# One stage each for output product, row norm and MLP in a two-block transformer kernel: tiles normed, turned and split one by one

## What is computed

```python
h = layer_norm(DN_ALPHA * h + mix, ln_mix_g[layer], ln_mix_b[layer])
h = layer_norm(DN_ALPHA * h + sq_relu_mlp(h, w_ff1[layer], w_ff2[layer]), ln_ffn_g[layer], ln_ffn_b[layer])
```

## Time and profile before

| what | value |
| --- | --- |
| median of 3 runs | 3636.25 us (3626.71 to 3639.91) |
| the profiled execution, its own time | 3637.71 us |
| its span, from first to last instruction | 3635.9 us |
| PE busy | 3322.3 us, 91% of the span |
| DVE busy | 1719.4 us, 47% |
| ACT busy | 841.4 us, 23% |
| POOL busy | 1112.7 us, 31% |
| mean granted clock of TensorE | 0.954 |

### The profile page before, as it was taken

One profiled execution on the slowest core, in us unless ns is written; L12 is line 12 of the kernel. 1 busy time (PEld: TensorE's weight loads), 2 busy tenths in 40 slices (PEclk: granted clock), 3 DMA queues, 4 the chain that ended last, 5 costly groups with the idle time before them and its releaser, 6 DMA issues. The chain is left out here.

```text
span 3635.9 us, 51954 instructions
## 1 busy us (share of the span) xinstructions
PE 3322.3 (91%) x20484; PEld 2927.8 (81%) x20484; DVE 1719.4 (47%) x3176; ACT 841.4 (23%) x1645; POOL 1112.7 (31%) x690
## 2 busy tenths in 40 slices
PE   8999999998988989799999995599998699999996
PEld 7898998887977879588888885588888688888885
DVE  4646465534776322633333347345553543333336
ACT  3545454412132110211111112133331111111110
POOL 5434343320195312523333303010001243333322
PEclk9999999888999999799999996799999799999998
DMA  6111111321001111211111101000001121111111
GB/s 192 52 46 47 46 47 52 151 60 41 30 14 38 58 33 37 81 47 46 46 47 57 58 0 36 8 22 14 10 4 58 34 71 46 46 48 55 46 35 47
DMA packets 179276, 173.28 MB, mean 48 GB/s; under 512 B 50267, under 2 KB 162331, under 8 KB 178971
## 3 DMA queue, kind: packets, MB, share of 16 engines
q1 hardware_dynamic: 177566, 170.70, 14.9%
q10 hardware_dynamic: 1568, 0.61, 0.1%
HBM read 157.30 MB, written 19.23 MB: 49 GB/s over the span
## 5 line engine op out<-in xcount | busy, mean ns | idle before, releaser
L2149 DVE TENSOR_TENSOR x<-x,banks 128x512 f32<-128x512 f32 x512 | 344.0, 684 | 210.3 <-PE banks L80 210.2
L78 PE MATMUL banks<-winbuf_hi,xt_hi 128*128 128x256 f32 x1024 | 302.1, 295 | 12.0 <-ACT qkn L950 7.5
L80 PE MATMUL banks<-winbuf_hi,xt_lo 128*128 128x256 f32 x1024 | 290.5, 284 | 0.0
L79 PE MATMUL banks<-winbuf_lo,xt_hi 128*128 128x256 f32 x1024 | 290.3, 284 | 0.0
L78 PEld LDWEIGHTS banks<-winbuf_hi,xt_hi 128*128 128x128 f32 x1024 | 196.5, 192 | 31.3 <-ACT qkn L950 11.5
L78 PE MATMUL banks<-h1t_hi,f1w_buf_hi 128*128 128x512 f32 x512 | 199.9, 390 | 2.7 <-PEq L2075 2.7
L78 PE MATMUL banks<-h3t_hi,f2w_buf_hi 128*128 128x512 f32 x512 | 199.9, 390 | 2.7 <-PEq L2075 2.7
L79 PE MATMUL banks<-h3t_lo,f2w_buf_hi 128*128 128x512 f32 x512 | 199.7, 390 | 0.0
L79 PE MATMUL banks<-h1t_lo,f1w_buf_hi 128*128 128x512 f32 x512 | 199.7, 390 | 0.0
L80 PE MATMUL banks<-h1t_hi,f1w_buf_lo 128*128 128x512 f32 x512 | 199.7, 390 | 0.0
L80 PE MATMUL banks<-h3t_hi,f2w_buf_lo 128*128 128x512 f32 x512 | 199.6, 390 | 0.0
(11 more groups left out here) (424 smaller groups left out, 8803.4 us busy)
## 6 DMA issues: line engine op xcount, KB each, us to landing
f1w_raw<-in_w_ff SPq DMA_DIRECT2D x32, 1024.0 KB, 5.2
f2w_raw<-in_w_ff SPq DMA_DIRECT2D x32, 1024.0 KB, 5.3
winraw<-in_w_in SPq DMA_DIRECT2D x128, 128.0 KB, 3.2
gluw_raw<-in_ssm_w_glu SPq DMA_DIRECT2D x16, 512.0 KB, 4.6
x<-in_x SPq DMA_DIRECT2D x8, 512.0 KB, 6.4
wow_raw<-in_w_out SPq DMA_DIRECT2D x4, 1024.0 KB, 5.1
x<-in_x SPq DMA_DIRECT2D x1, 4096.0 KB, 15.4
gew_raw<-in_w_ple_gate SPq DMA_DIRECT2D x4, 1024.0 KB, 5.0
```

The source lines that it names most:

```text
L78: nc.tensor.matmul(out, a.hi, b.hi, start=start, stop=False)
L79: nc.tensor.matmul(out, a.hi, b.lo, start=False, stop=False)
L80: return nc.tensor.matmul(out, a.lo, b.hi, start=False, stop=stop)
L2149: nc.vector.tensor_tensor(xx, xx, chip.ps[:, 4 + w % 4, :], ALU.add).then_inc(s_acc, 1)
```

## The change

`stage_product` and the "ln" kind of `stage_norm_transpose` are gone, and `stage_mlp` is one block that holds the output product (`Product`), the norm behind it (`RowNorm`), the MLP and the norm behind that. What remains of the old stage, `stage_transpose`, has its work unchanged for the callers that had no norm.

`RowNorm` works tile by tile. DVE takes the moments of tile j, makes variance plus epsilon, and centres the tile and multiplies it by the gain (`centre`). POOL takes the power for this tile alone, waits for ACT, and adds the shift (`root_and_shift`). ACT multiplies by the root (`scale`). PE turns tile j-2 behind the matmuls of tile j (`turn`), and `high_parts`, `low_parts` and `rescale` follow as before. POOL norms no tile by itself.

`Product` makes chunks 0 and 1 as before, and chunks 2 and 3 together, tile by tile, into one bank (512 columns), so that a tile's sum is complete after its 48 matmuls. Its weight has three buffers. Chunk 0 is loaded and split in the stage before: in the last part of the GLU (buffers at 160, 168, 184 and 144 KB) and in the last head of the attention.

In the MLP, hidden units 0 and 1 of chunk 0 need tiles 0 to 3 alone; they run before the turns of tiles 6 and 7. The first chunks of both MLP weights are loaded within the product. At the end, PE waits for all low parts of the last chunk, and then makes the two output units of a tile, with the turn of tile j-2 behind those of tile j. The first latent weight is loaded and split during the last chunk, the second once all hidden units are done, ahead of POOL's work for the norm. In the last norm each tile is stored once its shift is added. The addresses of several buffers move.

```diff
+    def centre(self, dve, j):
+        v, x = self.nc.vector, self.x
+        if j == 0:
+            dve.wait_ge(self.landed, 32)
+        if j >= 2:
+            dve.wait_ge(self.aggr, j - 1)
         for h in range(2):
-            self.nc.vector.bn_stats(self.st[:, h, :], x[:, j, h * HALF:(h + 1) * HALF]).then_inc(self.half, 1)
+            v.bn_stats(self.st[:, j % 2, h, :], x[:, j, h * HALF:(h + 1) * HALF]).then_inc(self.half, 1)
         dve.wait_ge(self.half, 2 * j + 2)
-        self.nc.vector.bn_aggr(self.mv[:, j, :], self.st[:, :, :].rearrange("p a s -> p (a s)")).then_inc(self.done, 1)
-        if j == NT - 1:
-            dve.wait_ge(self.done, NT)
+        v.bn_aggr(self.mv[:, j, :], self.st[:, j % 2, :, :].rearrange("p a s -> p (a s)")).then_inc(self.aggr, 1)
+        dve.wait_ge(self.aggr, j + 1)
+        v.tensor_scalar(self.rstd[:, j:j + 1], self.mv[:, j, 1:2], 1.0, LN_EPS, ALU.mult, ALU.add).then_inc(self.var, 1)
+        v.scalar_tensor_tensor(x[:, j, :], x[:, j, :], self.mv[:, j, 0:1], self.gtile[:, :],
+                               ALU.subtract, ALU.mult).then_inc(self.cen, 1)
+    def root_and_shift(self, pool, j):
+        g, x = self.nc.gpsimd, self.x
+        pool.wait_ge(self.var, j + 1)
+        g.tensor_tensor(self.rstd[:, j:j + 1], self.rstd[:, j:j + 1], self.chip.neghalf[:, :], ALU.pow).then_inc(self.root, 1)
+        pool.wait_ge(self.scaled, j + 1)
+        g.tensor_tensor(x[:, j, :], x[:, j, :], self.btile[:, :], ALU.add).then_inc(self.done, 1)
+    def scale(self, act, j):
+        act.wait_ge(self.root, j + 1)
+        act.wait_ge(self.cen, j + 1)
+        self.nc.scalar.activation(self.x[:, j, :], self.x[:, j, :], ACT.Copy,
+                                  scale=self.rstd[:, j:j + 1]).then_inc(self.scaled, 1)
+    def bank(self, j, q):
+        return self.chip.ps[:, self.banks[2 * (j % 2) + q], :]
+    def view(self, t, j, q):
+        if self.by_token:
+            return t[:, 4 * q:4 * q + 4, :].rearrange("p k (c j) -> p k c j", j=NT)[:, :, :, j]
+        return t[:, 4 * q:4 * q + 4, j * P:(j + 1) * P]
+    def turn(self, pe, j):
+        pe.wait_ge(self.done, j + 1)
+        if j >= 2:
+            pe.wait_ge(self.lo, 2 * j - 2)
+        for q in range(2):
+            for k in range(4):
+                last = self.nc.tensor.transpose(self.bank(j, q)[:, k * P:(k + 1) * P],
+                                                self.x[:, j, (4 * q + k) * P:(4 * q + k + 1) * P], self.chip.ident[:, :])
+            last.then_inc(self.turned, 1)
+    def high_parts(self, act, j):
+        for q in range(2):
+            act.wait_ge(self.turned, 2 * j + q + 1)
+            self.nc.scalar.activation(self.view(self.dst.hi, j, q), self.bank(j, q).rearrange("p (k c) -> p k c", k=4),
+                                      ACT.Copy).then_inc(self.hi, 1)
...
+    def rescale(self, act, j):
+        act.wait_ge(self.turned, 2 * j + 2)
+        self.nc.scalar.mul(self.x[:, j, :], self.x[:, j, :], ALPHA).then_inc(self.again, 1)
+    def low_parts(self, dve, j):
+        for q in range(2):
+            dve.wait_ge(self.hi, 2 * j + q + 1)
+            self.nc.vector.tensor_tensor(self.view(self.dst.lo, j, q), self.bank(j, q).rearrange("p (k c) -> p k c", k=4),
+                                         f32(self.view(self.dst.hi, j, q)), ALU.subtract).then_inc(self.lo, 1)
 def token_rows(t, h, j):
...
+    CHUNKS = D // CH
+    WIDE = 2
...
+    def sync(self, sp):
+        for n in range(1, self.CHUNKS):
+            self.ws.load(sp, n)
+    def pool(self, pool):
+        self.ws.do_split(pool, 1, 1)
+        self.ws.do_split(pool, 2, 2)
+        self.ws.do_split(pool, 3, 0, (self.mm, NT))
+    def tile(self, out, n, b, j):
+        for k in range(KT):
+            last = mm3(self.nc, out, self.rows.at(slice(None), k, slice(j * P, j * P + P)),
+                       self.ws.bufs[b].at(slice(None), k, slice(None)), k == 0, k == KT - 1)
+        return last
+    def pe(self, pe):
+        ps, norm = self.chip.ps, self.norm
+        for n in range(2):
+            pe.wait_ge(self.ws.split, n + 1)
+            for j in range(NT):
+                if n:
+                    pe.wait_ge(self.added, j + 1)
+                self.tile(ps[:, j, 0:CH], n, n, j).then_inc(self.mm, 1)
+        pe.wait_ge(self.ws.split, 4)
+        for j in range(NT):
+            pe.wait_ge(self.added, NT + j + 1 if j < 4 else self.narrow + j - 3)
+            self.tile(ps[:, j % 4, 0:CH], 2, 2, j)
+            self.tile(ps[:, j % 4, CH:2 * CH], 3, 0, j).then_inc(self.mm, 1)
+            if j == 2:
+                pe.wait_ge(self.added, self.narrow)
+            if j >= 2:
+                norm.turn(pe, j - 2)
+    def act(self, act):
+        for j in range(NT):
+            if j >= 2:
+                self.norm.high_parts(act, j - 2)
+            self.norm.scale(act, j)
+            if j >= 2:
+                self.norm.rescale(act, j - 2)
+        for j in (NT - 2, NT - 1):
+            self.norm.high_parts(act, j)
+            self.norm.rescale(act, j)
+    def dve(self, dve):
+        def add(u, cols, bank):
+            dve.wait_ge(self.mm, u + 1)
+            xx = self.x[:, u % NT, cols]
+            self.nc.vector.scalar_tensor_tensor(xx, xx, self.x_scale, bank, ALU.mult, ALU.add).then_inc(self.added, 1)
+        for u in range(self.narrow):
+            n, j = u // NT, u % NT
+            add(u, slice(n * CH, (n + 1) * CH), self.chip.ps[:, j, 0:CH])
+        for j in range(NT):
+            add(self.narrow + j, slice(HALF, D), self.chip.ps[:, j % 4, :])
+            dve.wait_ge(self.added, self.narrow + j + 1)
+            self.norm.centre(dve, j)
+            if j >= 2:
+                self.norm.low_parts(dve, j - 2)
+        for j in (NT - 2, NT - 1):
+            self.norm.low_parts(dve, j)
...
             ws.load_all(sp, KT)
+            sp.wait_ge(ws.split, KT)
+            then.load(sp, 0, first=True)
         @block.gpsimd
         def _(pool):
             ws.split_all(pool, KT, s_mm, 2)
+            then.do_split(pool, 0, 0, (s_mm, 2 * KT - 2))
...
+            product.sync(sp)
+            ws1.load(sp, 0, first=True)
+            sp.wait_ge(product.ws.split, product.CHUNKS)
             ws2.load(sp, 0, first=True)
+            sp.wait_ge(product.mm, product.narrow)
+            first.load(sp)
             with sp.Fori(1, NB) as n:
                 ws1.load(sp, n)
                 ws2.load(sp, n)
-            moments.load(sp)
+            norm.load(sp)
+            if latent is not None:
+                sp.wait_ge(s_m1, U1 * (NB - 1))
+                latent.load(sp, 0)
+                sp.wait_ge(s_m1, U1 * NB)
+                sp.wait_ge(ws2.split, NB)
+                latent.load(sp, 1)
+            if store is not None:
+                for j in range(NT):
+                    sp.wait_ge(norm.done, j + 1)
+                    sp.dma_start(store[:, j, :], x[:, j, :]).then_inc(norm.stored, 16)
+                sp.wait_ge(norm.stored, 16 * NT)
         @block.gpsimd
         def _(pool):
-            ws2.do_split(pool, 0, 0)
...
+            product.pool(pool)
+            ws1.do_split(pool, 0, 0)
+            for j in range(NT):
+                first.root_and_shift(pool, j)
+            ws2.do_split(pool, 0, 0, (product.mm, product.narrow + NT))
             ws1.do_split(pool, 1, 1)
...
+            if latent is not None:
+                latent.do_split(pool, 0)
+                latent.do_split(pool, 1)
+            for j in range(NT):
+                norm.root_and_shift(pool, j)
...
+            pe.wait_ge(ws1.split, 1)
+            pe.wait_ge(product.added, product.narrow + NT - 2)
+            pe.wait_ge(first.lo, NT)
+            hidden_unit(0, 0, 0)
+            first.turn(pe, NT - 2)
+            hidden_unit(0, 0, 1)
+            first.turn(pe, NT - 1)
+            pe.wait_ge(product.added, product.narrow + NT)
+            pe.wait_ge(first.lo, 2 * NT)
+            hidden_unit(0, 0, 2)
+            hidden_unit(0, 0, 3)
...
+            pe.wait_ge(ws2.split, NB)
+            pe.wait_ge(s_alo, U1 * NB + 2)
+            pe.wait_ge(s_sq, U1 * NB + 4)
+            for j in range(NT):
+                output_unit(NB - 1, 1, 2 * j)
+                output_unit(NB - 1, 1, 2 * j + 1)
+                if norm.dst is not None and j >= 2:
+                    norm.turn(pe, j - 2)
+            if norm.dst is not None:
+                norm.turn(pe, NT - 2)
+                norm.turn(pe, NT - 1)
...
+            for j in range(NT):
+                if norm.dst is not None and j >= 2:
+                    norm.high_parts(act, j - 2)
+                norm.scale(act, j)
+                if norm.dst is not None and j >= 2:
+                    norm.rescale(act, j - 2)
+            if norm.dst is not None:
+                for j in (NT - 2, NT - 1):
+                    norm.high_parts(act, j)
+                    norm.rescale(act, j)
...
+            for j in range(NT):
+                add(NB - 1, 2 * j)
```

(36 more changed lines are left out.)

329 lines of the change are left out of this document (85 added, 244 removed).

## The result

The changed kernel takes 3530.0 us, the median of four runs (3529.2 to 3531.3); the kernel before takes 3638.1 beside it (four runs, 3626.7 to 3640.3). The ratio is 0.971, with a 95% interval of 0.969 to 0.973. That is 108 us less, where 91.5 were forecast. The profiled executions have spans of 3635.9 and 3529.5 us, a difference of 106.4.

The account below looks back on a forecast made before the run. PE, busy for 91% of the span, bounds the kernel, so gains come only where it stands still. Four sites sum to 44 + 43 + 10 - 5.5 = 91.5 us, from 3636.25 to 3545; range 3525 to 3582.

Parts of the forecast that it names:

- site 4: Last norm, from the last hidden unit to the end: 57.2 us before, forecast 5.5 us slower.
- Site 1: From the GLU's last matmul to the end of hidden unit 4: 172.2 us to 128.1, gain 44.
- Site 2: From the attention to hidden unit 4 of the second MLP: 171.1 us to 126.9, gain 43 after 1 for the last head.
- site 3: From the last hidden unit to the latents: 77.1 us before, gain 10; best case 18, worst 0.
- 2.0 for 16: In the first product: cost in us of PE changing its kind of work around 16 turns, 0.12 each.
- Then POOL is the bound: Norm ahead of the latents: POOL's loop sets 5.1 us a tile, 6.2 where a centring goes ahead of the power.
- shift 3.20: POOL's shift of one tile takes 3.20 us, read from the earlier trace; in the last norm part of 6.15 a tile.
- DVE becomes the bound of the product: Rival: in the product each centring waits for a whole shift, 8.4 us a tile instead of 6.9; 3569 us, chance 0.10.
- The early weights aren't early: Rival: chunk 0 splits or the latents' second weight come late, one 11 us gap stays; 3558 us, chance 0.06.
- The ring is quicker in the tails: Rival: POOL's ring takes 5.1 us a tile ahead of the latents and in the last norm; 3531 us, chance 0.05.
- The ring locks PE: Rival: in the products neighbouring tiles' loops don't overlap, 18.1 us a tile instead of 6.9; 3724 us, slower, chance 0.03.
- The clock: Rival: transposes between the products' matmuls let PE's clock fall to 0.50, costing 106 us; 3651, no change, chance 0.02.

Follow-up runs that it names:

- run 3: Changed kernel with each turn in the product one tile behind instead of two; 3550.0 us, ratio 0.977 to the kernel before.
- run 1: Changed kernel with the first chunk of both output weights loaded and split at the product's start again; 3546.6 us, ratio 0.975 to the kernel before.
- run 6: Changed kernel with high and low parts ahead of the latents written in plain order instead of to every 8th column; 3518.1 us, ratio 0.968 to the kernel before.
- run 8: Changed kernel with DVE waiting for a tile's power before centring it, in all four norms; 3530.2 us, ratio 0.969 to the kernel before.
- Run 5: Changed kernel with the second latent weight's split moved into the latents' own block, on POOL; 3522.6 us, ratio 0.969 to the kernel before.
- Run 7: Changed kernel with POOL's power of tile j+1 ahead of the shift of tile j in the last norm; 3527.5 us, ratio 0.970 to the kernel before.
- Run 9: Changed kernel with the last norm's shift on DVE instead of POOL; 3531.0 us, ratio 0.970 to the kernel before.
- run 4: Changed kernel with the second latent weight's split behind POOL's shifts for the norm, instead of ahead of them; 3529.6 us, ratio 0.971 to the kernel before.

## Why the prediction was right, and where it was not

**The total** is inside the range; the forecast was 15 us too high. 10.4 of it is site 4, 2.6 sites 1 and 2, and 3.9 a stretch that isn't the change's; against it stand 1.0 at the latents and the attention, 0.7 at site 3 and 0.3 in the loops.

**Site 1: right, 1.8 us too long.** Gap 3.3 (forecast 3.6), wait ahead of the third hidden unit 1.6 (1.5), 64 transposes at full clock. The term "2.0 for 16" changes of PE's kind of work was mis-sized: it is nothing. A pair of chunks with its turn takes 6.62 us, which is 2 x 2.88 + 0.86, and PE is busy for the whole stretch. The gap cost no clock, as forecast (1.00 from 1343 to 1351 us); that it was too short for that isn't shown, since a wait of 2.1 us in run 3 did cost clock. That the norm keeps up held, with a path of 7.7 us instead of 8.7; run 3 showed that two tiles of distance are what covers it, and run 1 that the early split has its cover.

**Site 2: right.** The gap was 2.0 (2.4), and the last head grew by 1.3 where 1 was taken; run 1 gives it back.

**Site 3: the right sum by a wrong step.** The start was right (first power at T + 16 against T + 17, behind the second latent weight). "Then POOL is the bound" fell: only the first three tiles are POOL's (5.1 us); from then on DVE's round of 6.2 us sets the pace, because its two low parts of a tile are strided and take 2.2 us and not the 1.3 taken from the plain ones of the product, and because PSUM adds, moments and centring stand behind them. Runs 6 and 8 show it from both sides. 6.2 was forecast as a number, for the first five or six tiles, with another reason; the prediction made no sum of DVE's work at this site, and that the total came out right is luck. Run 5 shows the term that could be taken away, the split ahead of the norm (11 us in the forecast, 9.5 measured), and that it was worth 6.5.

**Site 4: wrong in sign.** Forecast 5.5 slower, measured 4.9 faster. The last shift was to end at T + 57.3 and ended at T + 49.4 (3526.5 - 3477.2), and the rest of 2.5 is the tail. The step that failed is "shift 3.20", from the earlier trace rows: that instruction had itself waited. The record of DVE ahead of it, in the kernel before, is this:

```profile
3611.52 3.36 DVE L214 SCALAR_TENSOR_TENSOR x<-x,meanvar,gain 128x1024 f32<-128x1024 f32 x1
```

It ended at 3614.88, one microsecond behind the beginning that the earlier trace rows give for POOL's shift. By itself a shift takes 2.40; with 0.2 of handoffs that were not there, a tile's "6.15" is 5.15, and eight tiles make the 8 us. The tail was taken as 5.5 from the kernel before, and is 3.0. The stores differ there. The last issues of the kernel before, and the time from issue to landing over its eight stores:

```profile
3630.44 1.57 SPq L188 DMA_DIRECT2D out<-x  x3
...
DMA to landing us min/median/max: 2.6/2.6/4.2
```

and of the kernel after:

```profile
3526.53 0.33 SPq L2051 DMA_DIRECT2D out<-x  x1
...
DMA to landing us min/median/max: 2.6/2.6/2.6
```

In the kernel before three stores were issued within 1.6 us at the end, and the last one took 4.2 us to land; in the kernel after a single one is left. This is read from the traces, and no run tried it. The forecast's own condition, that a centring gets in each time a shift ends, was right. Run 7 shows the bound: POOL's ring, which stands for ACT's scale in every turn; once it no longer does, DVE's 4.1 us of work a tile set the pace.

**The rivals.** *DVE becomes the bound of the product*: refuted, since no centring there took over 1.28 us. The distance was as small as forecast only for the first tiles (0.4 us from the end of a shift to the next centring) and 1.3 later. *The early weights aren't early*: refuted. Run 1 is a kernel in which they are late, and it is 16.6 us slower than the kernel after. *The ring is quicker in the tails*: its number came true at site 4, 5.1 a tile, and its time, 3531, is within 1 us of the measured one, both by luck. Its reason was that no centring gets in ahead of a power; there each one did, the shift was cheaper, and at site 3 a tile took 6.2. *The ring locks PE*: refuted, since two tiles' loops overlap (6.62 us a tile, no wait for a shift) even with one tile of distance (run 3). *The clock*: 1.00 with eight transposes behind every 48 matmuls. The Trainium skill ("TensorE: Matmul & The Clock Gate", Part 4) has transposes not counted as PE's activity; these 54 us don't speak for a price of that.

**The Trainium skill's rule on adds** ("GPSIMD Engine Reference", Engine selection) would put the shift on VectorE. The prediction worked out 15 us for a norm from it. Run 9 tried it where it could matter most: DVE's shift is indeed half as long (1.22 against 2.40 us), and the norm is 1.3 us shorter, not 8 times the difference. An engine's price for one instruction isn't the price of the place, where the other engine has no time left.

## What to carry to other kernels

A norm between two products costs PE little more than its transposes (0.86 us a tile) once it works tile by tile and its turns stand so far behind the sums that the path fits between them: measure the path from sum to last write (7.7 us here), divide it by a tile's matmuls (5.8), round up, and keep PE's independent work for the last tiles, where a wait also costs clock. At the tails, where PE has no more work, ask which engine's round is the longest before moving an instruction, and give POOL's unrelated work a place behind the next meeting of all engines, not only behind the norm. And a duration read where two engines use SBUF at once holds waiting: look for the same instruction with nothing beside it.

## What the runs showed of the hardware that was not expected

- A POOL instruction on one column (128x1) takes 0.55 us alone and 1.52 us when a DVE instruction with two inputs in SBUF has begun just before it (1412.64 and 1412.81 above); the waiting is inside the recorded duration. The same holds the other way: a centring of 1.28 us took 2.28 behind a shift and 7.38 behind a split of 6.73. The Trainium skill ("SBUF — State Buffer", Who interferes with whom) describes an exclusive lock on the pair of ports that DVE and GpSimd share, kept for a whole instruction by the one that starts first; run 8, where only the order changed, agrees with its 0.55 us.
- When both wait, DVE's centring got in ahead of POOL's next instruction each time, though POOL had nothing between its two (the shift of 3503.72 ended at 3506.11, the centring at 3507.20, the power recorded from 3506.07 at 3507.60).
- DVE's low parts of two halves take 1.28 us written plainly and 2.2 us to every 8th column; that is the 0.9 us by which a tile of site 3 is shorter in run 6. DVE is the bound with either: 6.2 us a tile against 5.34, and 5.1 for POOL's ring.
- A wait of 2.8 us on PE costs clock in some executions and not in others. All the kernels from the change on have it between the last hidden unit and the next output unit (behind f1a_lo above at site 3, behind f2a_lo at site 4). At site 4 the clock stayed at full speed in six of the eleven profiled executions and fell in five; at site 3 it fell in ten. In the kernel after the clock at site 4 stayed at full speed, in run 4's it fell to a mean of 0.63, and the first tile's sum came 2.5 us later; this is what the two lengths of site 4 are (the first power comes 8.3 to 8.4 us behind the last relu in the six, 9.7 to 10.8 in the five). The stretch from the last relu to the first tile's sum, of the kernel after:

```profile
3477.16:3483.00 5.84, 3.04 (x13) 2.55 (x14) 2.07 (x3) 1.22 (x2) 0.00 (x0) 1.00 0.00 0
```

  and of run 4's kernel:

```profile
3479.80:3488.10 8.30, 5.49 (x13) 4.37 (x14) 2.06 (x3) 1.23 (x2) 0.00 (x0) 0.63 0.00 0
```

- Executions differ by up to 16 us in their first 1340 us, where these kernels do the same work but for one early load and split; what a run says of a few microseconds has to be read from its stretches.
